# Attention core: the odd head's softmax rows normalised on GpSimd, the even head's on VectorE

## The chip, the cores and the metric

One NeuronCore of one Trainium2 chip runs the whole program. The metric is device time in microseconds (us) of one launch; the runs shown are compared by their median. The engines are TensorE (PE in the rows; PEld is its weight load), VectorE (DVE), ScalarE (ACT), GpSimd (POOL) and SyncE (SP), which here only issues transfers.

## What is computed

A two-layer encoder over 272 tokens (16 learned meta tokens and 256 others) of 1024 channels. Layer 0 holds grouped-query attention, layer 1 a recurrent block, and each is wrapped in two SwiGLU FFNs. The change lies in the attention of layer 0: 16 query heads of 64 channels, 4 key/value heads, full softmax over all 272 keys.

```
def attention_mixer(x, w_qkv, q_gain, k_gain, w_o, cos, sin):
    ...
    q = apply_rope(rms_norm(q, q_gain), cos, sin) * (HEAD_DIM ** -0.5)
    k = apply_rope(rms_norm(k, k_gain), cos, sin)
    def attend(qb):
        s = jnp.einsum('bqhgd,bkhd->bhgqk', qb, k).astype(jnp.float32)
        p = jax.nn.softmax(s, axis=-1).astype(v.dtype)
        return jnp.einsum('bhgqk,bkhd->bqhgd', p, v)
    ...
    return o @ w_o
```

## The kernel before

Every engine has its own written-out instruction stream, in order; semaphores tie them together. There is no scheduler: the order of the Python calls is the order on the engine.

The attention core is a loop of 18 steps (`STEPS`), nine for each pair of key/value heads. Step 0 and step 9 take the last 16 tokens of four head pairs at once and have one score tile of 128 rows by 272 keys; each of the other 16 steps takes 128 tokens of two heads, and so has two tiles, an even one and an odd one, which sit next to each other in `prow`, the SBUF buffer of the softmax rows. `prow` has four slots, two per step, used by turns. In all there are 34 tiles.

What one step s does, and where:

- TensorE `scores(s)` (L793): the scores into PSUM. From step 3 on it is issued two steps ahead, and waits until the exponents of step s-2 are out.
- VectorE `maximum(s)` (L1768) and `shifted(s)` (L1776): row maxima times the query's factor.
- ScalarE `exponents(s)` (L1292): one exponential per tile, from PSUM to `prow`, each with its row sum by an accumulator read.
- VectorE `inverse(s)` (L1781): the reciprocals `rinv` of the row sums of the step's tiles, one instruction; it raises the semaphore `p_inv`.
- VectorE `normalise(s)` (L1788): `prow` times `rinv`, one instruction per tile, each raising `p_norm`.
- TensorE `turn(s)` (L807): six small transposes per tile into PSUM. It waits on `p_norm` before each tile.
- ScalarE `place(s)` (L1314, L1308 for steps 0 and 9): copies the turned tiles to `pt`.
- TensorE `weigh(s)` (L819): the turned weights times the values. When the second half of a head pair is done, VectorE `out_split` (L1792, L1794) takes the result out of PSUM as a high part `xh` and a low part `xl`, and TensorE must wait for that (`o_ready`) before the next pair's first `weigh`.

The order on each engine: TensorE runs `scores(s+2)`, `turn(s)`, `weigh(s-1)`. ScalarE runs `exponents(s+1)`, `place(s)`. VectorE runs `normalise(s)`, then `out_split` in steps 4, 6, 8, 10, 13, 15 and 17, then `maximum(s+2)`, `inverse(s+1)`, `shifted(s+2)`. In steps 16 and 17 TensorE runs parts of the output projection (`begin_wo`) in place of scores. GpSimd does the rotary additions ahead of the core, and after it `restore(1)`, whose wait ends later; in the core it has no work.

Of the kernel before, what the change touches and what calls it, by code (L numbers as in the profile page):

```python
# [9 lines left out]
ALU = mybir.AluOpType  # L10
# [65 lines left out]
STEPS = NKV // 2 * STEPS_S  # L76
# [3 lines left out]
def first_tile(step):  # L80

    p, q = divmod(step, STEPS_S)
    return COLUMNS * p + max(0, 2 * q - 1)


def turning():
# [65 lines left out]
def build(nc, x, meta, gains, ffn_in, ffn_out, w_qkv, q_gain, k_gain, w_o, rec_in, conv_w, conv_b,  # L152
          gate_w, gate_b, lam, rec_out, consts, out):
    ctx = ExitStack()
    with ctx:  # L155
        def sb(name, shape, dt=F32):
            return ctx.enter_context(nc.sbuf_tensor(name, shape, dt))

        def sem(name):
            return ctx.enter_context(nc.semaphore(name))  # L160
# [40 lines left out]
        rinv = sb("rinv", [P, NKV // 2 * COLUMNS])  # L201
        prow = sb("prow", [P, 4, L])
# [47 lines left out]
        def row_parts(t):  # L250

            a = row_start(t)
            if t % 2:
                return (a, slice(0, 2 * P)), (a - META, slice(2 * P, L))
            return ((a, slice(0, L)),)
# [4 lines left out]


        gates_used = sem("gates_used")
        s_in, s_vec = sem("gains_landed"), sem("vectors_landed")
        table_loaded, warm_set = sem("table_loaded"), sem("warm_set")
        s_rope = sem("rotary_tables_landed")
# [16 lines left out]
        s_done, nmax_ready, p_exp, p_inv, p_norm, t_done, pt_ready, pv_done, oh_ready, o_ready = (sem(n) for n in (  # L282
            "s_done", "nmax_ready", "p_exp", "p_inv", "p_norm", "t_done", "pt_ready", "pv_done", "oh_ready", "o_ready"))
# [194 lines left out]
        def _(pe):  # L478
# [251 lines left out]
            def attention():  # L730
# [44 lines left out]
                def scores(s):  # L775

                    p, q = divmod(s, STEPS_S)
                    if s >= 2:
                        pe.wait_ge(p_exp, first_tile(s - 1))
                    dst = SCORE[s % 2]  # L780
                    if q == 0:
                        pe.wait_ge(q_roped, KT_N + 4 * p + 4)
                        for g in range(GROUP):
                            j, o = 2 * p + g // 2, HD * (g % 2)
                            last = pe.matmul(dst[32 * g:32 * g + 32, 0, 0:L], qt_row[o:o + HD, 2 * L * j + 2 * P:2 * L * j + 2 * P + 2 * META],
                                             kd[o:o + HD, j, :], start=True, stop=True)
                    else:
                        j, i, half = pair_of(s)
                        for keys in (slice(0, L // 2), slice(L // 2, L)):
                            for e in range(2):  # L790
                                o = HD * e
                                a = 2 * L * j + row_start(i) + P * half
                                last = pe.matmul(dst[:, e, keys], qt_row[o:o + HD, a:a + P],  # L793
                                                 kd[o:o + HD, j, keys], start=True, stop=True)
                    last.then_inc(s_done, 1)

                def turn(s):

                    banks, placed = TURN[s]
                    if placed:  # L800
                        pe.wait_ge(pt_ready, placed)
                    for e, tile in enumerate(range(first_tile(s), first_tile(s + 1))):
                        pe.wait_ge(p_norm, tile + 1)
                        for c, k0 in enumerate(KTOK):
                            for rows, b in zip((slice(0, HD), slice(HD, P)), banks):
                                o = HD * (3 * e + c)
                                last = pe.transpose(flipped[0:KT, b, o:o + HD], prow[rows, 2 * (s % 2) + e, k0:k0 + KT], ident[rows, rows])  # L807
                        last.then_inc(t_done, 1)
# [98 lines left out]
            def begin_wo(k0, k1):  # L907

                pe.wait_ge(w_ready, U_WO + 1)
                if k0 == 0:  # L910
                    pe.wait_ge(p_exp, first_tile(STEPS - 1))
                for k in range(k0, k1):
                    pe.wait_ge(o_ready, k + 1)
                    for m in range(2):
                        product(bank[PROJ_BANKS[1][0][m]][:, 0:L], U_WO, 2 * k + m, xh[:, k, :], xl[:, k, :], k == 0, False)
# [559 lines left out]
        def _(dve):  # L1475
# [214 lines left out]
            def attention():  # L1690
# [92 lines left out]
                def normalise(s):  # L1783
                    a, n = first_tile(s), first_tile(s + 1) - first_tile(s)
                    dve.wait_ge(p_inv, s + 1)
                    for e in range(n):
                        v = prow[:, 2 * (s % 2) + e, :]
                        dve.tensor_scalar(v, v, rinv[:, a + e:a + e + 1], None, ALU.mult).then_inc(p_norm, 1)  # L1788

                def out_split(pair):  # L1790
                    dve.wait_ge(pv_done, pair + 1)
# [215 lines left out]
        @block.gpsimd  # L2007
        def _(pool):
            def restore(n):

                t0 = PROJ_T0[n]
                pool.wait_ge(root_inverted, n)
                pool.wait_ge(x_ready, 8 * n + 8)
                pool.wait_ge(hsq_ready, 8 * n + 8)
                for c in range(KC):
                    pool.tensor_tensor(h[:, c, t0:L], h[:, c, t0:L], root[:, t0:L], ALU.mult).then_inc(h_restored, 1)  # L2016

            def rotary():
                def times_cos(t):
                    pool.wait_ge(q_gained, t + 1)  # L2020
                    if t >= 2:
                        pool.wait_ge(q_roped, t - 1)
                    pool.tensor_tensor(qc[:, t % 2, :], qp[:, t % 2, :], cos, ALU.mult).then_inc(q_cos, 1)

                def roped(t):
                    pool.wait_ge(q_sin, t + 1)
                    pool.wait_ge(q_cos, t + 1)
                    if t < KT_N:
                        last = pool.tensor_tensor(qn[:, t, :], qc[:, t % 2, :], pad[:, t % 2, 0:L], ALU.add)
                    for a, cols in row_parts(t) if t >= KT_N else ():  # L2030
                        a += 2 * L * ((t - KT_N) // 2)
                        n = cols.stop - cols.start
                        last = pool.tensor_tensor(qt_row[:, a:a + n], qc[:, t % 2, cols], pad[:, t % 2, cols], ALU.add)
                    last.then_inc(q_roped, 1)

                pool.wait_ge(s_rope, 16)
                pool.wait_ge(hacc_step, 8 * 1 + 8)
                for t in range(QKT):
                    times_cos(t)
                    if t == KT_N + 3:  # L2040
                        pool.wait_ge(q_final, KT_N)
                        pool.dma_start(kd[HD:P, 0:NKV:2, :], kd[0:HD, 0:NKV:2, :]).then_inc(k_dup, 16)
                        pool.dma_start(kd[0:HD, 1:NKV:2, :], kd[HD:P, 1:NKV:2, :]).then_inc(k_dup, 16)
                    roped(t)

            def recurrent():
                def gated_input(n):
                    for d in range(2):
                        pool.wait_ge(sig_done, 8 * n + 4 * d + 4)
                        v = gi[:, n % BLOCKS_HELD, d]  # L2050
                        pool.tensor_tensor(v, v, xc[:, n], ALU.mult).then_inc(ix_done, 1)

                def y_sum(n):
                    pool.wait_ge(scan_done, 4 * n + 4)
                    pool.tensor_tensor(ys[:, 2 * n:2 * n + 2, :], gw[:, n % BLOCKS_HELD, 0], gw[:, n % BLOCKS_HELD, 1], ALU.add).then_inc(ysum_done, 1)

                def y_gated(n):
                    pool.wait_ge(gelu_done, n + 1)
                    pool.wait_ge(ysum_done, n + 1)
                    s, t = slice(2 * n, 2 * n + 2), slice(PROJ_T0[4], L)  # L2060
                    pool.tensor_tensor(ys[:, s, t], ys[:, s, t], mg[:, s, t], ALU.mult).then_inc(y_full, 1)

                gated_input(0)
                gated_input(1)
                y_sum(0)
                gated_input(2)
                y_sum(1)
                y_gated(0)
                y_gated(1)
                gated_input(3)  # L2070
                y_sum(2)
                y_gated(2)

            rotary()
            restore(1)
            restore(2)
            restore(3)
            recurrent()
            restore(4)
# [26 lines left out]
```

## Time and profile before

| | us |
|---|---|
| median of 3 runs | 1049.96 (1049.76 to 1050.05) |
| the profiled execution, its own time | 1050.0 |
| its span | 1048.2 |
| PE busy (share of the span) | 1035.1 (99%) |
| DVE busy | 694.6 (66%) |
| ACT busy | 552.2 (53%) |
| POOL busy | 80.9 (8%) |

The granted TensorE clock was 0.999 of full speed. Busy time says how long an engine had an instruction in hand. In the timelines, a row begins with the start and the length; with "x2" the length is that of both together. Instructions of an engine are pipelined, so one may start a little before the row before it has ended. Brackets hold the idle time of the engine ahead of a row and who ended it. The attention core runs from about 268 to 300 us, and what is left of it overlaps the output projection up to 310 us.

### The profile page before, as it was taken

What the parts mean: (1) busy time and instruction counts of PE and PEld (TensorE: products, weight loads), DVE (VectorE), ACT (ScalarE), POOL (GpSimd) and SP (SyncE); (2) the same over time, 40 slices, a digit from 0 to 9 for tenths busy, and PEclk for the clock granted to TensorE, in tenths of its full rate; (3) what the DMA queues carried; (4) which work ended last, traced back from release to release, by engine and by line L of the source; (5) the groups of instructions that cost most, each with busy time, mean ns of one, the idle gap of its engine ahead of it and who ended that gap; (6) DMA issues with size and microseconds to landing.
All of it is one profiled execution on the core that took longest, in us unless ns stands there. A gap on an engine that the chain in (4) does not pass through costs nothing. (4 is left out here: it accounts for less than half of the span.)

```text
span 1048.2 us, 20625 instructions
## 1 busy us (share of the span) xinstructions
PE 1035.1 (99%) x8416; PEld 1010.2 (96%) x8416; DVE 694.6 (66%) x1008; ACT 552.2 (53%) x818; POOL 80.9 (8%) x76
## 2 busy tenths in 40 slices
PE   9999999999999999999999999999999999999997
PEld 8999999999789999999999999999999999999886
DVE  6766656478868866665487666554788687676652
ACT  6544454467875544444455444444568764544641
POOL 0000000008004000003000000030022320000000
PEclk9999999999999999999999999999999999999999
DMA  9654446635104365435746554466237426656531
GB/s 308 209 188 160 142 151 204 217 105 176 63 3 160 124 198 187 154 111 191 230 132 200 164 160 146 153 198 216 91 111 252 161 83 202 199 165 233 180 125 40
DMA packets 161200, 170.16 MB, mean 162 GB/s; under 512 B 3313, under 2 KB 154153, under 8 KB 161129
## 3 DMA queue, kind: packets, MB, share of 16 engines
q1 hardware_dynamic: 160744, 168.70, 49.5%
q8 instruction: 51, 0.84, 0.3%
q0 software_dynamic: 96, 0.28, 0.1%
q10 hardware_dynamic: 288, 0.18, 0.1%
q14 instruction: 21, 0.16, 0.0%
HBM read 167.82 MB, written 1.05 MB: 161 GB/s over the span
## 5 line engine op out<-in xcount | busy, mean ns | idle before, releaser
L1480 DVE TENSOR_TENSOR wl<-raw,wh 128x2048 fp32r<-128x2048 f32 (+2 forms) x164 | 342.4, 2108 | 147.1 <-ACT wh L1024 146.8
L483 PE MATMUL bank<-xh,wl 128*128 128x272 f32 (+1 forms) x1492 | 431.8, 289 | 0.1
L485 PE MATMUL bank<-xh,wh 128*128 128x272 f32 (+1 forms) x1492 | 428.6, 287 | 0.0
L484 PE MATMUL bank<-xl,wh 128*128 128x272 f32 (+1 forms) x1492 | 427.1, 286 | 0.0
L1024 ACT ACTIVATE wh<-raw 128x2048 fp32r<-128x2048 f32 (+3 forms) x163 | 280.4, 1744 | 107.7 <-PE bank L485 82.1
L483 PEld LDWEIGHTS bank<-xh,wl 128*128 128x128 f32 x1492 | 281.1, 188 | 1.9 <-issue 1.2
L485 PEld LDWEIGHTS bank<-xh,wh 128*128 128x128 f32 x1492 | 281.1, 188 | 0.0
L484 PEld LDWEIGHTS bank<-xl,wh 128*128 128x128 f32 x1492 | 281.1, 188 | 0.0
L484 PE MATMUL bank<-al,wh 128*128 128x272 f32 x528 | 152.2, 288 | 0.0
L483 PE MATMUL bank<-ah,wl 128*128 128x272 f32 x528 | 152.2, 288 | 0.0
L485 PE MATMUL bank<-ah,wh 128*128 128x272 f32 x528 | 151.4, 287 | 0.0
L1102 ACT ACTIVATE tmp<-tmp 128x272 f32<-128x272 f32 (+1 forms) x88 | 37.5, 427 | 207.3 <-DVE tmp L1575 207.1
L484 PEld LDWEIGHTS bank<-al,wh 128*128 128x128 f32 x528 | 99.3, 188 | 0.0
L485 PEld LDWEIGHTS bank<-ah,wh 128*128 128x128 f32 x528 | 99.2, 188 | 0.0
L483 PEld LDWEIGHTS bank<-ah,wl 128*128 128x128 f32 x528 | 99.2, 188 | 0.0
L1594 DVE TENSOR_TENSOR al<-tmp,ah 128x272 f32 (+3 forms) x88 | 38.2, 438 | 51.7 <-ACT ah L1107 51.1
L1575 DVE TENSOR_TENSOR tmp<-bank,r 128x272 f32<-128x272 f32 (+1 forms) x88 | 38.0, 432 | 45.3 <-PE bank L485 45.2
L2016 POOL TENSOR_TENSOR h<-h,root 128x272 f32<-128x272 f32 (+1 forms) x32 | 35.5, 1144 | 419.9 <-DVE root L1512 419.9
L1107 ACT ACTIVATE ah<-tmp 128x272 f32 (+3 forms) x88 | 37.4, 429 | 47.7 <-DVE tmp L1584 47.7
L1584 DVE TENSOR_TENSOR tmp<-tmp 128x272 f32<-128x272 f32 (+1 forms) x88 | 38.2, 437 | 13.9 <-ACT tmp L1102 11.5
L504 PE MATMUL bank<-xh,wl 128*128 128x272 f32 (+1 forms) x172 | 44.9, 289 | 1.2 <-ACT xh L1030 1.0
L505 PE MATMUL bank<-xh,wh 128*128 128x272 f32 (+1 forms) x172 | 44.5, 287 | 0.0
(206 smaller groups left out, 1146.4 us busy)
## 6 DMA issues: line engine op xcount, KB each, us to landing
raw<-in_ffn_w_in SPq DMA_DIRECT2D x87, 1024.0 KB, 5.3
raw<-in_ffn_w_out SPq DMA_DIRECT2D x24, 768.0 KB, 4.6
raw<-in_ffn_w_out SPq DMA_DIRECT2D x24, 640.0 KB, 3.9
raw<-in_ffn_w_out SPq DMA_DIRECT2D x10, 1024.0 KB, 5.2
raw<-in_rec_w_in SPq DMA_DIRECT2D x8, 1024.0 KB, 5.5
raw<-in_attn_w_qkv SPq DMA_DIRECT2D x6, 1024.0 KB, 5.0
raw<-in_attn_w_o SPq DMA_DIRECT2D x4, 1024.0 KB, 5.6
raw<-in_rec_gate_w SPq DMA_DIRECT2D x16, 256.0 KB, 5.1
```

Of the source, the lines that this page charges most:

```text
L483: pe.matmul(dst, b, mh, start=first, stop=False)
L484: pe.matmul(dst, a, ml, start=False, stop=False)
L485: return pe.matmul(dst, a, mh, start=False, stop=last)
L504: pe.matmul(dst, b, xh[:, k, t0:L], start=k == 0, stop=False)
L505: pe.matmul(dst, a, xh[:, k, t0:L], start=False, stop=False)
L1024: act.activation(wh[:, slot(u), 0:kn * 256], raw[:, slot(u), 0:kn * 256], ACT.Copy).then_inc(wh_ready, units)
L1102: act.activation(sl[:, b, t0:L], gp[:, b, t0:L], ACT.Silu).then_inc(silu_done, 1)
L1107: act.activation(ah[:, m, t0:L] if isinstance(it, int) else ah[:, bass.ds(4 * it + m, 1), t0:L].rearrange("p a l -> p (a l)"), aa[:, b, t0 ...
L1480: dve.tensor_tensor(wl[:, slot(u), 0:kn * 256], w, wh[:, slot(u), 0:kn * 256].bitcast(F32), ALU.subtract).then_inc(w_ready, units)
L1575: dve.tensor_tensor(gp[:, b, t0:L], bank[banks[0]][:, t0:L], r[:, t0:L], ALU.mult).then_inc(gate_scaled, 1)
L1584: dve.tensor_tensor(aa[:, b, t0:L], sl[:, b, t0:L], up[:, b, t0:L], ALU.mult).then_inc(a_full, 1)
L1594: dve.tensor_tensor(d, aa[:, b, t0:L], s, ALU.subtract).then_inc(a_ready, 1)
```

## The change

`normalise(s)` on VectorE now does only the even tile, and counts steps in `p_norm`. A new function on GpSimd, `normalise_odd(s)`, does the odd tile of the 16 steps that have one; it waits for the same `p_inv`, and raises a semaphore of its own, `p_norm_odd`. TensorE's `turn(s)` waits for `p_norm` before the even tile's six transposes and for `p_norm_odd` before the odd tile's six. The two buffers, the arithmetic and the order of everything else are as before. GpSimd runs all its 16 instructions between the rotary part and `restore(1)`.

```
+def odd_tiles(steps):
+    return first_tile(steps) - steps
...
                     for e, tile in enumerate(range(first_tile(s), first_tile(s + 1))):
-                        pe.wait_ge(p_norm, tile + 1)
+                        if e == 0:
+                            pe.wait_ge(p_norm, s + 1)
+                        else:
+                            pe.wait_ge(p_norm_odd, odd_tiles(s + 1))
...
                 def normalise(s):
                     a, n = first_tile(s), first_tile(s + 1) - first_tile(s)
                     dve.wait_ge(p_inv, s + 1)
-                    for e in range(n):
-                        v = prow[:, 2 * (s % 2) + e, :]
-                        dve.tensor_scalar(v, v, rinv[:, a + e:a + e + 1], None, ALU.mult).then_inc(p_norm, 1)
+                    v = prow[:, 2 * (s % 2), :]
+                    dve.tensor_scalar(v, v, rinv[:, a:a + 1], None, ALU.mult).then_inc(p_norm, 1)
...
+            def normalise_odd(s):
+                if first_tile(s + 1) - first_tile(s) == 2:
+                    pool.wait_ge(p_inv, s + 1)
+                    v = prow[:, 2 * (s % 2) + 1, :]
+                    t = first_tile(s) + 1
+                    pool.tensor_scalar(v, v, rinv[:, t:t + 1], None, ALU.mult).then_inc(p_norm_odd, 1)
+
             rotary()
+            for s in range(STEPS):
+                normalise_odd(s)
             restore(1)
```

VectorE before, from the normalisation of step 4 (with its `out_split`) to that of step 6:

```order
L1788 TENSOR_SCALAR prow<-prow,rinv 128x272 x2
L1792 CAST xh<-weighed 128x272
L1794 TENSOR_TENSOR xl<-weighed,xh 128x272
L1768 TENSOR_REDUCE nmax<-score_even 128x2
L1781 RECIPROCAL rinv<-rsum 128x2
L1776 TENSOR_TENSOR shift<-nmax,hq 128x2
L1788 TENSOR_SCALAR prow<-prow,rinv 128x272 x2
L1768 TENSOR_REDUCE nmax<-score_odd 128x2
```

VectorE after, the same stretch (all line numbers are 8 or 9 higher):

```order
L1796 TENSOR_SCALAR prow<-prow,rinv 128x272
L1800 CAST xh<-weighed 128x272
L1802 TENSOR_TENSOR xl<-weighed,xh 128x272
L1777 TENSOR_REDUCE nmax<-score_even 128x2
L1790 RECIPROCAL rinv<-rsum 128x2
L1785 TENSOR_TENSOR shift<-nmax,hq 128x2
L1796 TENSOR_SCALAR prow<-prow,rinv 128x272
L1777 TENSOR_REDUCE nmax<-score_odd 128x2
```

One of the two multiplications of each step has gone from VectorE; nothing else has moved there. GpSimd after, from the end of the rotary part to `restore(1)`:

```order
L2031 TENSOR_TENSOR tmp<-tmp,cst 128x272 [waits q_roped,q_gained]
L2041 TENSOR_TENSOR qt<-tmp,pad 128x256 [waits q_cos,q_sin]
L2041 TENSOR_TENSOR qt<-tmp,pad 128x16
L2087 TENSOR_SCALAR prow<-prow,rinv 128x272 [waits p_inv] x16
L2024 TENSOR_TENSOR h<-h,root 128x272 [waits hsq_ready,x_ready,root_inverted]
```

The row with x16 is new; before, the additions of `restore(1)` followed the rotary part directly.

## Rows read from the trace of the kernel before

**Rows 1.** The page's first part: busy time, share of span, instructions.

```profile
PE 1035.1 (99%) x8416; PEld 1010.2 (96%) x8416; DVE 694.6 (66%) x1008; ACT 552.2 (53%) x818; POOL 80.9 (8%) x76
```

**Rows 2.** Busy by stretch: PE, PEld, DVE, ACT, POOL; PEclk, DMA share, GB/s.

```profile
272.80:282.40 9.60, 8.69 (x152) 7.47 (x152) 8.65 (x30) 9.44 (x26) 0.00 (x0) 1.00 0.01 3
272.80:300.40 27.60, 25.12 (x422) 20.64 (x422) 24.61 (x82) 25.91 (x73) 0.00 (x0) 1.00 0.01 2
300.40:310.00 9.60, 9.60 (x105) 8.43 (x104) 2.18 (x8) 4.67 (x8) 0.00 (x0) 1.00 0.01 2
```

**Rows 3.** ScalarE's timeline around steps 4 to 6: start, length, instruction.

```profile
276.43 0.59 ACT L1292 ACTIVATE prow<-score_odd,shift,hq 128x272 f32<-128x272 f32 x1
...
277.53 0.82 ACT L1314 ACTIVATE pt<-flipped 96x768 f32<-96x768 f32 x1
278.41 0.58 ACT L1292 ACTIVATE prow<-score_even,shift,hq 128x272 f32<-128x272 f32 x1
```

**Rows 4.** VectorE's timeline from the normalisation of step 4 to step 6's.

```profile
276.09 0.63 DVE L1788 TENSOR_SCALAR prow<-prow,rinv 128x272 f32<-128x272 f32 x2
276.64 0.43 DVE L1792 CAST xh<-weighed 128x272 fp32r<-128x272 f32 x1
277.10 0.44 DVE L1794 TENSOR_TENSOR xl<-weighed,xh 128x272 fp32r<-128x272 f32 x1
...
278.09 0.15 DVE L1781 RECIPROCAL rinv<-rsum 128x2 f32<-128x2 f32 x1
278.21 0.16 DVE L1776 TENSOR_TENSOR shift<-nmax,hq 128x2 f32<-128x2 f32 x1
278.29 0.63 DVE L1788 TENSOR_SCALAR prow<-prow,rinv 128x272 f32<-128x272 f32 x2
279.28 0.72 DVE L1768 TENSOR_REDUCE nmax<-score_odd 128x2 f32<-128x544 f32 x1 [0.36 <-PE score_odd L793]
...
280.12 0.63 DVE L1788 TENSOR_SCALAR prow<-prow,rinv 128x272 f32<-128x272 f32 x2
280.66 0.43 DVE L1792 CAST xh<-weighed 128x272 fp32r<-128x272 f32 x1
```

**Rows 5.** TensorE's timeline in the same cycle, and the core's last wait.

```profile
277.69 0.88 PE L819 MATMUL weighed<-pt,vt 96*64 96x128 f32 x12 [0.40 <-DVE xl L1794]
278.50 0.73 PE L793 MATMUL score_odd<-kd,qt 64*128 64x136 f32 x8
279.06 0.50 PE L807 MATMUL flipped<-cst,prow 64*96 64x64 f32 x12
279.50 0.96 PE L819 MATMUL weighed<-pt,vt 96*64 96x144 f32 x12
...
299.60 0.88 PE L819 MATMUL weighed<-pt,vt 96*64 96x128 f32 x12 [0.26 <-DVE xl L1794]
```

**Rows 6.** Line L1788 alone: durations in ns, min/median/max, and its span.

```profile
L1788 DVE TENSOR_SCALAR prow<-prow,rinv x34: 353/356/363, 268.5 to 302.1; 128x272 f32<-128x272 f32 x34
```

**Rows 7.** VectorE's timeline where GpSimd works beside it.

```profile
242.99 0.43 DVE L1724 TENSOR_TENSOR pad<-bank,cst 128x272 f32<-128x272 f32 x1
...
245.30 0.78 DVE L1713 TENSOR_TENSOR hq<-hq,rc_q 128x4 f32<-128x4 f32 x1
246.00 2.28 DVE L1480 TENSOR_TENSOR wl<-raw,wh 128x2048 fp32r<-128x2048 f32 x1
...
779.20 1.68 DVE L1857 TENSOR_SCALAR xc<-pad,vec_b 128x272 f32<-128x272 f32 x2
```

**Rows 8.** GpSimd's timeline at the same places.

```profile
243.50 0.90 POOL L2033 TENSOR_TENSOR qt<-tmp,pad 128x256 f32<-128x256 f32 x2 [2.67 <-DVE pad L1724]
...
245.29 0.77 POOL L2033 TENSOR_TENSOR qt<-tmp,pad 128x272 f32<-128x272 f32 x1
246.01 2.90 POOL L2023 TENSOR_TENSOR tmp<-tmp,cst 128x272 f32<-128x272 f32 x1
...
779.05 1.34 POOL L2051 TENSOR_TENSOR gi<-gi,xc 128x544 f32<-128x544 f32 x1 [7.99 <-ACT gi L1339]
```

More of the change, by code:

```diff
@@ L262, in build @@
         gates_used = sem("gates_used")
+        p_norm_odd = sem("odd_tile_normalised")
         s_in, s_vec = sem("gains_landed"), sem("vectors_landed")
```

## Prediction

> **What bounds the kernel now.** I first read the page's busy shares: TensorE is busy for 99% of the span [rows 1]. So nothing that VectorE, ScalarE or GpSimd does in this kernel counts, unless it shortens or lengthens a wait of TensorE. The second view is the busy time by stretch. In one part of the attention core TensorE is busy for 8.69 us of 9.60, and ScalarE for 9.44; over the whole core from 272.8 to 300.4 TensorE is busy for 25.12 of 27.60; from 300.4 us on for 9.60 of 9.60 [rows 2]. The core is thus the place where TensorE waits, and whatever is won or lost there moves the start of the output projection at 300.4 us by as much, and with it the end of the kernel.
>
> Third, the timelines of one cycle, to see which wait ends last. ScalarE's part of a step is two exponentials and a copy: exponential at 276.43, copy at 277.53, which is 1.10 later, and from copy to the next exponential 0.70 where nothing holds it. That is a floor of 1.80 us for a step. The next exponential came at 278.41, so this step took 1.98 [rows 3]. It was held by the row maximum's product `shift`, which ended at 278.21 + 0.16 = 278.37 [rows 4].
>
> Why was `shift` late? Steps with an `out_split` form a loop that runs through two steps. In step 4: normalise 276.09, cast 276.64, `xl` 277.10 and its end at 277.54 [rows 4]; TensorE, idle for 0.40, starts `weigh` at 277.69 and the next scores at 278.50, ending at 279.23 [rows 5]; VectorE, idle for 0.36, takes the maximum at 279.28, then the reciprocal, and normalises step 6 at 280.12 [rows 4]. The period is 280.12 - 276.09 = 4.03 us for two steps, against ScalarE's floor of 3.60. The two multiplications of `normalise` are in this loop, ahead of the cast. The last such wait is the 0.26 us at 299.60 [rows 5], right ahead of the projection.
>
> **What goes from VectorE.** One tile takes 0.356 us, two tiles 0.63 [rows 4, 6], so 0.63 - 0.36 = 0.27 us go in each of 16 steps, 4.3 us of VectorE time in all. Only six of the seven steps with an `out_split` have it on TensorE's path (4, 6, 8, 10, 13, 15; that of step 17 comes when TensorE has the projection's products to do). In the others VectorE has idle time, or ScalarE's floor holds.
>
> **What is late next.** In step 6 the cast cannot start before `weigh(4)` has ended: 279.50 + 0.96 = 280.46, and it started at 280.66 [rows 4, 5]. With some 0.05 us for the hand-over it may come at 280.51, so 0.15 of the 0.27 can be taken there and no more. Written as a loop on TensorE, from scores(7) to scores(9): 278.50 to the end of `weigh(4)` 1.96, hand-over 0.05, cast 0.46, `xl` 0.44, hand-over 0.15, `weigh(5)` 0.81. Sum 3.87 against 4.03: 0.16 us per two steps is all that this loop gives.
>
> **What comes to GpSimd.** No row shows a multiplication by a column of scalars there. Nearest rows: an addition of two 128x272 tiles takes 0.77 us, one of 128x544 1.34 [rows 8]; the difference is 0.57 for 272 columns, so about 0.20 is fixed. An upper bound in kind is hard to give: a form with a scalar operand could be slower than the two-tensor form. From below, VectorE's own 0.356 for this very tile [rows 6] bounds it. I take 0.5 to 0.77, since only one tensor is read, and work the sum with 0.77 and with 0.5; for the range I also price 1.2.
>
> The Trainium skill (GPSIMD Engine Reference, Engine selection) says that operations with one input run on GpSimd at roughly line rate, which would be an estimate of some 0.4 us for this tile; no row here shows it. By it the sum would come out at the favourable end below.
>
> **The hand-overs and the port.** GpSimd starts about 0.08 us after VectorE's result: 242.99 + 0.43 = 243.42, start 243.50 [rows 7, 8]. VectorE itself goes on from its reciprocal sooner: 278.09 + 0.15 = 278.24, normalise at 278.29 [rows 4], which is 0.05. So the even multiplication starts some 0.03 us ahead of the odd one. They can't run side by side. At 245.30 a VectorE instruction on 4 columns took 0.78, because GpSimd had started at 245.29; at 246.00 VectorE started 0.01 ahead, and the GpSimd addition behind it took 2.90 in place of 0.77 [rows 7, 8]. That multiplications by a scalar column are hit too shows at 779.20: two took 1.68 while a GpSimd instruction begun at 779.05 ran for 1.34 [rows 7, 8]; the two heads' multiplication rows are of the same kind and size. So I let the odd tile start when the even one is done. In the pair at 246 us GpSimd ended at 248.91, 0.63 after VectorE's end at 248.28, which makes 0.14 of its 0.77 overlap. The odd tile is then ready at 0.36 + 0.63 + 0.06 (to TensorE) = 1.05 us after the even one's start if it costs 0.77, and at 0.78 if it costs 0.5. Before it was ready at 0.63.
>
> **What this does to the transposes.** In step 5 the odd tile was ready at 278.29 + 0.63 = 278.92, and its six transposes are the second half of those that start at 279.06, that is at about 279.30 [rows 4, 5]. With 1.05 it is ready at 279.34, which is late by 0.04; with 0.78 it is early. So the loop is 3.91 to 3.87 us long, and 0.12 to 0.16 shorter than before. In steps where the normalisation starts close to its scores the same 1.05 makes the odd transposes up to 0.3 us late (step 2, step 11: multiplication at about the time at which scores start). `place` is then just in time, but `weigh` and the scores behind it on TensorE start 0.3 later, and the first `out_split` of each half, in steps 4 and 13, loses nearly all its gain.
>
> **The sum.** With 0.77: steps 4 to 8 give about 0.07 us, steps 13 and 15 together about 0.17; in all -0.24. With 0.5: the first steps give 0.24 and the next 0.10 before TensorE's loop takes over, and some 0.04 of it is lost again in step 8, so -0.30; the second half gives 0.27 in step 13 and 0.16 in step 15, -0.43; in all -0.73. I take the middle on the cautious side, -0.4 us. Nothing after 300.4 us depends on the odd tiles of steps 16 and 17: their transposes stand behind products of the projection there, over 2 us long. `restore(1)` waits for other work until long after. The profiled execution took 1050.0 us, with a span of 1048.2, and the median is 1049.96, so both sums agree to 0.04. Forecast: 1049.96 - 0.4 = 1049.6 us.
>
> **Rivals.** First, GpSimd gets the port first. The margin is 0.03 us, and the multiplication must first read its scalar, so it may ask for the port later than its start says. Then the even tile waits for about 0.62 us of GpSimd's 0.77 (the 4-column instruction: 0.78 less its own 0.16), and is done 1.05 us after the reciprocal in place of 0.68 for both tiles before. That is about +0.4 in each two-step cycle, since the cast stands behind it: six cycles, +2.4 us, with little change in the steps at ScalarE's floor. Time 1052.3; with a GpSimd instruction of 0.5 us, +0.1 per cycle, no loss to be seen. This is the case on the other side, and its point of decision is which of the two starts first, with a GpSimd multiplication above 0.7 us. Against it stand the two pairs of rows above, in which the start order decided down to 0.01 us. The Trainium skill (SBUF — State Buffer, Who interferes with whom) has it as a rule: an instruction of VectorE in a two-port mode and one of GpSimd exclude each other, and whichever issues first keeps the shared ports for the whole instruction. By that rule, the trace agrees: 1.68 us for two multiplications.
>
> Second, the GpSimd multiplication is slow, 1.2 us. Then the loop above is 0.43 longer than 3.91, so +0.3 against before in each of four cycles; and the steps at ScalarE's floor are caught as well: exponentials to reciprocal to odd tile to transposes to copy to exponentials is about 3.6 us for two steps at 0.77 and 4.0 at 1.2, which costs 0.4 in each of three such pairs. Sum about +2.4, time 1052.4. From about 0.9 us on the change brings nothing.
>
> Third, nearly all of TensorE's idle time in the core goes. It is 27.60 - 25.12 = 2.48 us [rows 2], so a gain that can be seen, over 2.1 us, would have to take it nearly whole, the waits at ScalarE's floor with it. Time 1047.8; I give it little.
>
> **How the numbers follow.** A measurement of this kernel can tell about 0.2%, 2.1 us, from no change. My case, within 1 us of before, has 0.60. GpSimd first has 0.20, half of it beyond +2.1 us. The slow multiplication has 0.17, also half of it beyond. The whole gain has 0.03. That makes faster by over 0.2% 0.03, slower 0.19, and 0.78 within. The likeliest case alone spans 1049.1 to 1050.2. For 8 in 10 the range must reach into both slow cases, and leaves out their far ends: 1048.9 to 1052.3.
>
> **What would show it.** Right: L1796 at 18 instructions of 0.36 us; 16 GpSimd multiplications that start at VectorE's and last 0.9 at most, its wait included; the pair from normalise to the cast shrunk from 0.55 to 0.3; the period from step 4 to step 6 at 3.9; the projection's first product at 300.0 in place of 300.4. Wrong: even multiplications of 0.8 or more (GpSimd first), transposes that wait for GpSimd by more than 0.1 in most steps, or GpSimd rows above 1.2 us.

## The result

The changed kernel takes 1051.16 us (median of 20 runs, 1050.88 to 1053.59) against 1049.93 of the kernel before (20 runs, 1049.33 to 1050.44): ratio 1.0013, 95% interval 1.0007 to 1.0019. It is 1.2 us slower. The forecast was 0.4 us faster: the time lies in the stated range of 1048.9 to 1052.3, but the sign is the wrong one, and the likeliest case did not come.

The profiled execution took 1051.19 us with a span of 1049.4. The page's first part, to be read against [rows 1]:

```profile
PE 1036.2 (99%) x8416; PEld 1010.6 (96%) x8416; DVE 690.8 (66%) x992; ACT 552.8 (53%) x818; POOL 101.5 (10%) x92
```

VectorE lost 16 instructions, as worked out, and 3.8 us where 4.3 was worked out. GpSimd gained 16 instructions and 20.6 us; the 16 rows themselves make 17.9 of it, and the gate multiplications of layer 1, far behind the core, the other 2.7 (14.7 in place of 12.0). The two multiplication lines of the changed kernel (ns, min/median/max):

```profile
L1796 DVE TENSOR_SCALAR prow<-prow,rinv x18: 354/358/568, 268.4 to 303.0; 128x272 f32<-128x272 f32 x18
L2087 POOL TENSOR_SCALAR prow<-prow,rinv x16: 963/1131/1134, 269.5 to 303.0; 128x272 f32<-128x272 f32 x16
```

The second line is the answer in short. GpSimd needs 0.96 us for the odd tile where it starts first (step 4 alone), and 1.13 where it starts behind VectorE (the other 15). The median of VectorE's even multiplication stayed at 0.36, so GpSimd does not hold VectorE up in most steps. TensorE's timeline, at step 2 and from step 5 on, answers to [rows 5]:

```profile
272.90 0.38 PE L816 MATMUL flipped<-cst,prow 64*96 64x64 f32 x6 [0.46 <-ACT pt L1323]
273.64 0.37 PE L816 MATMUL flipped<-cst,prow 64*96 64x64 f32 x6 [0.36 <-POOL prow L2087]
273.94 0.88 PE L828 MATMUL weighed<-pt,vt 96*64 96x128 f32 x12
...
278.83 0.73 PE L799 MATMUL score_odd<-kd,qt 64*128 64x136 f32 x8
279.40 0.84 PE L816 MATMUL flipped<-cst,prow 64*96 64x64 f32 x12
280.17 0.96 PE L828 MATMUL weighed<-pt,vt 96*64 96x144 f32 x12
...
301.58 0.40 PE L489 MATMUL bank<-xh,wl 128*128 128x272 f32 x1
```

In step 2 the twelve transposes fall apart into six and six, with GpSimd named between them. In step 5 they take 0.84 in place of 0.50, and `weigh(4)` starts 1.34 us after the scores instead of 1.00. The projection's first product comes at 301.58; before it came at 300.41. Where the core begins on the time axis differs by up to 0.3 us between the traced executions, ahead of all that the change touches, so from here on I count from the core's first normalisation, that of step 0:

```profile
268.52 0.36 DVE L1788 TENSOR_SCALAR prow<-prow,rinv 128x272 f32<-128x272 f32 x1
300.41 0.39 PE L483 MATMUL bank<-xh,wl 128*128 128x272 f32 x1
```

before, and in the changed kernel

```profile
268.36 0.36 DVE L1796 TENSOR_SCALAR prow<-prow,rinv 128x272 f32<-128x272 f32 x1
```

From there to the projection it is 31.89 us before and 33.22 in the changed kernel: 1.33 us more, so the whole loss lies in the core. Counted in the same way, the normalisation comes 0.56 us later in step 4, 0.95 in step 9, 0.94 in step 10 and 1.30 in step 13. So about 0.9 of the 1.33 us arise at the start of the two halves (steps 2 to 4 and 11 to 13), and 0.4 in the cycles of the first half.

VectorE's timeline from step 4 to step 6, against [rows 4], and GpSimd's:

```profile
276.17 0.16 DVE L1790 RECIPROCAL rinv<-rsum 128x2 f32<-128x2 f32 x1
...
276.49 0.57 DVE L1796 TENSOR_SCALAR prow<-prow,rinv 128x272 f32<-128x272 f32 x1
276.98 0.43 DVE L1800 CAST xh<-weighed 128x272 fp32r<-128x272 f32 x1
...
278.43 0.15 DVE L1790 RECIPROCAL rinv<-rsum 128x2 f32<-128x2 f32 x1
278.55 0.16 DVE L1785 TENSOR_TENSOR shift<-nmax,hq 128x2 f32<-128x2 f32 x1
278.63 0.36 DVE L1796 TENSOR_SCALAR prow<-prow,rinv 128x272 f32<-128x272 f32 x1
...
280.45 0.36 DVE L1796 TENSOR_SCALAR prow<-prow,rinv 128x272 f32<-128x272 f32 x1
281.17 0.44 DVE L1800 CAST xh<-weighed 128x272 fp32r<-128x272 f32 x1 [0.36 <-PE weighed L828]
```

```profile
276.42 0.96 POOL L2087 TENSOR_SCALAR prow<-prow,rinv 128x272 f32<-128x272 f32 x1 [1.11 <-DVE rinv L1790]
278.68 1.13 POOL L2087 TENSOR_SCALAR prow<-prow,rinv 128x272 f32<-128x272 f32 x1 [1.30 <-DVE rinv L1790]
```

VectorE did get its time back, and now spends it waiting: before the cast at 281.17 it stands idle for 0.36 us, because `weigh(4)`, pushed back by the odd transposes, has not ended. From cast to cast the cycle lasts 281.17 - 276.98 = 4.19 us; before, 280.66 - 276.64 = 4.02 [rows 4]. Two waits, summed over the kernel (engine, what it waited for: us in total, times, longest), show the exchange. In the changed kernel:

```profile
PEld flipped L816 <- POOL prow L2087: 1.9, 6, 0.5
PE weighed L828 <- DVE xl L1802: 0.2, 1, 0.2
```

and before:

```profile
PE weighed L819 <- DVE xl L1794: 1.4, 4, 0.5
```

The wait for `xl` fell from 1.4 us to 0.2. In its place the transposes' weight loads wait 1.9 us for GpSimd. (Not all of either is lost time: what counts is the 1.33 us by which the core is longer.)

### The profile page after: what moved, and what is told of

The parts are those of the page before. It is cut to its first block and busy times, and to the rows that moved or that the text cites. A ratio compares the mean times of both kernels' runs of the same rounds, so it can differ in the third digit from the quotient of the medians.

```text
span 1049.4 us, 20625 instructions
## 1 busy us (share of the span) xinstructions
PE 1036.2 (99%) x8416; PEld 1010.6 (96%) x8416; DVE 690.8 (66%) x992; ACT 552.8 (53%) x818; POOL 101.5 (10%) x92
## 3 DMA queue, kind: packets, MB, share of 16 engines
HBM read 167.82 MB, written 1.05 MB: 161 GB/s over the span
```

## The experiments

Three theories were to be told apart. *Late tile*: GpSimd delivers the odd tile too late. *Port*: VectorE and GpSimd hold each other up. *Hand-over*: the second semaphore and the split wait themselves cost something. The comparison in each case is with the kernel before, run on the same chip in the same job (1049.89, 1049.84 and 1049.81 us in the three jobs). The intervals of most of these single comparisons are some 0.9 us to either side, so for differences below 1 us I also take from the trace the stretch from the core's first normalisation to the projection's first product (31.89 us before). It rests on one execution of each kernel. All diffs are against the changed kernel.

**Semaphores alone.**

```
                     dve.tensor_scalar(v, v, rinv[:, a:a + 1], None, ALU.mult).then_inc(p_norm, 1)
+                    if n == 2:
+                        v = prow[:, 2 * (s % 2) + 1, :]
+                        dve.tensor_scalar(v, v, rinv[:, a + 1:a + 2], None, ALU.mult).then_inc(p_norm_odd, 1)
...
-            for s in range(STEPS):
-                normalise_odd(s)
```

> VectorE does both tiles again, one instruction each, but the odd one raises its own semaphore and TensorE waits on two semaphores in turn; GpSimd does nothing in the core. Late tile (the loss comes from when GpSimd delivers the odd tile): as before, 1049.9, within 0.2 us. Port (VectorE and GpSimd block each other): also as before. Hand-over (the second semaphore and the split wait cost something themselves): about 1051, as the change.

Measured: 1050.06 us, ratio 1.0001 (0.9992 to 1.0010), and the stretch is 31.91 us against 31.89. The hand-over costs nothing that can be seen.

**The odd tile left out.**

```
-                        else:
-                            pe.wait_ge(p_norm_odd, odd_tiles(s + 1))
...
-            for s in range(STEPS):
-                normalise_odd(s)
```

> The odd tile is not normalised at all, so that half of the weights keep their row sums; VectorE does the even tile alone and TensorE waits for nothing else. This is the change with a multiplication on GpSimd that costs nothing. Late tile: the gain of the shorter VectorE chain stands alone, between 0.4 and 0.9 us faster than before, about 1049.2. If the shorter chain is worth nothing, 1049.9. Hand-over and port say nothing here.

Measured: 1049.32 us, ratio 0.9995 (0.9986 to 1.0004). The time alone does not prove a gain; the trace has a stretch of 31.34 us (268.44 to 299.78), 0.55 shorter than before, which agrees with the medians (0.57):

```profile
299.78 0.40 PE L489 MATMUL bank<-xh,wl 128*128 128x272 f32 x1
```

So the shorter VectorE chain is worth about 0.6 us when no odd tile is late. One part of the gain is missing even here: in step 4 the even multiplication starts 0.32 us after its reciprocal has ended, in place of 0.04 before, and the cast comes no sooner than before. In this kernel GpSimd has no work, so it is not GpSimd's doing:

```profile
275.81 0.17 DVE L1788 RECIPROCAL rinv<-rsum 128x2 f32<-128x2 f32 x1
...
276.30 0.36 DVE L1794 TENSOR_SCALAR prow<-prow,rinv 128x272 f32<-128x272 f32 x1 [0.24 <-issue]
```

**The odd tile left out, GpSimd busy beside.**

```
+        idle = sb("idle", [P, L])
...
-                        else:
-                            pe.wait_ge(p_norm_odd, odd_tiles(s + 1))
...
+                    pool.wait_ge(idle_step, odd_tiles(s) + 1)
-                    pool.tensor_scalar(v, v, rinv[:, t:t + 1], None, ALU.mult).then_inc(p_norm_odd, 1)
+                    pool.tensor_scalar(idle[:, :], idle[:, :], rinv[:, t:t + 1], None, ALU.mult).then_inc(idle_step, 1)
```

> As the run without the odd tile (which stays unnormalised), but GpSimd multiplies a tile of the same size that nobody reads, at the same moments and with the same scalar column. Late tile: within 0.3 us of the run without the odd tile, since nobody waits for GpSimd. Port: as slow as the change, about 1051, since VectorE's instructions are held up in the same way.

Measured: 1049.60 us, ratio 0.9998 (0.9989 to 1.0007). Its two lines show the same load on GpSimd as in the change, and VectorE hardly touched:

```profile
L1796 DVE TENSOR_SCALAR prow<-prow,rinv x18: 354/358/416, 268.4 to 301.2; 128x272 f32<-128x272 f32 x18
L2087 POOL TENSOR_SCALAR idle<-idle,rinv x16: 962/1132/1135, 269.6 to 301.3; 128x272 f32<-128x272 f32 x16
```

The stretch is 31.39 us, 0.05 more than without GpSimd. So what GpSimd does to VectorE in this form costs between 0.05 (trace) and 0.3 us (medians), and what is left, from 1049.60 to the change's 1051.16, is TensorE's wait for the tile. That does not clear the port: of the 1.13 us after which the tile is ready, 0.17 are what GpSimd loses behind VectorE, and the next runs show what 0.17 us are worth there.

**Less and more of the tile.** Half of the columns:

```
-                    v = prow[:, 2 * (s % 2) + 1, :]
+                    v = prow[:, 2 * (s % 2) + 1, 0:L // 2]
```

> GpSimd multiplies only the left 136 of the odd tile's 272 columns; the right half stays unnormalised. Its instruction should take about 0.6 us in place of 0.96. Late tile: the odd tile is ready 0.4 us sooner, the transposes wait in hardly any step, and the time falls to 1049.3 to 1049.7. Port: VectorE is held up only where GpSimd starts first, and the time falls by less than 0.3 us from 1051.2.

204 columns, the same edit with `0:204`:

> GpSimd multiplies the left 204 of the odd tile's 272 columns; the rest stays unnormalised. By the two sizes measured the instruction takes 0.82 us alone and 0.99 behind VectorE's, which is what the prediction had put in for the whole tile. Late tile, with the prediction's sum: 1049.6 to 1049.8. If the loss grows from the first tenth of lateness on, halfway between the half tile and the change, about 1050.3.

Half a tile more:

```
+                    pool.tensor_scalar(v[:, 0:L // 2], v[:, 0:L // 2], rinv[:, t:t + 1], None, ALU.mult).then_inc(idle_step, 1)
+                    pool.wait_ge(idle_step, odd_tiles(s) + 1)
                     pool.tensor_scalar(v, v, rinv[:, t:t + 1], None, ALU.mult).then_inc(p_norm_odd, 1)
```

> As the change, but ahead of each odd tile GpSimd also multiplies the left half of that tile by itself (that half is then normalised twice), so that the tile is ready about 0.65 us later. Late tile: each of the 14 steps in the loop is held by TensorE's wait for GpSimd; the two-step period grows by about 0.65, in all 4 to 7 us more than the change, 1055 to 1058. Port: VectorE's own instructions are held a little more, under 1 us more.

Measured, with the time from GpSimd's start to the tile's end behind a VectorE that started first (for the last row 271.56 - 269.71, two instructions), and with the stretch of the trace:

| odd tile on GpSimd | ready after (us) | time (us) | against before | stretch against 31.89 |
|---|---|---|---|---|
| none | - | 1049.32 | -0.57 | -0.55 |
| 136 columns | 0.79 | 1049.47 | -0.42 | -0.39 |
| 204 columns | 0.96 | 1050.11 | +0.30 | +0.43 |
| 272 columns (the change) | 1.13 | 1051.16 | +1.23 | +1.33 |
| 136 and 272 | 1.85 | 1055.35 | +5.51 | +5.37 |

The ratios of the three new kernels are 0.9996 (0.9987 to 1.0005), 1.0003 (0.9994 to 1.0012) and 1.0055 (1.0042 to 1.0069): of these times only the last is clear of before by itself; the other two rest on the trace beside them.

```profile
L2087 POOL TENSOR_SCALAR prow<-prow,rinv x16: 677/792/795, 269.5 to 301.3; 128x136 f32<-128x136 f32 x16
```

```profile
L2087 POOL TENSOR_SCALAR prow<-prow,rinv x16: 792/960/963, 269.7 to 302.2; 128x204 f32<-128x204 f32 x16
```

Up to 0.79 us nearly all of the gain is kept. From 0.96 on each 0.1 us of lateness costs some 0.6 us: (1055.35 - 1051.16) / (1.85 - 1.13) = 5.8, about one lateness per two-step cycle. This fits the loop in which the odd transposes stand once. The run with 204 columns also prices the port: it delivers after 0.96 us, when the whole tile would be ready if VectorE did not stand in its way, and is 1.05 us faster than the change. By this estimate most of the change's 1.23 us hang on the last 0.17. Late tile and port are thus one chain: VectorE delays GpSimd, and GpSimd's tile delays TensorE. In the slowest of these kernels the wait for GpSimd is the long one:

```profile
PEld flipped L817 <- POOL prow L2090: 6.7, 11, 1.2
```

**Another form on GpSimd.**

```
-                    pool.tensor_scalar(v, v, rinv[:, t:t + 1], None, ALU.mult).then_inc(p_norm_odd, 1)
+                    pool.tensor_tensor(v, v, rinv[:, t:t + 1].broadcast_to([P, L]), ALU.mult).then_inc(p_norm_odd, 1)
```

> As the change, but GpSimd multiplies the odd tile by a two-tensor multiplication whose second operand is the scalar column broadcast along the row. If that form takes the 0.77 us of the additions, the odd tile comes 0.2 us sooner than in the change. Late tile: the time falls to about 1049.7 to 1050.3. Port: a form that reads two tensors from SBUF blocks VectorE no less; no change from 1051.2, or slower.

Measured: 1051.51 us, ratio 1.0015 (1.0006 to 1.0024). The expectation by the late tile failed, though its premise was more than met: the instruction takes 0.64 us. What it does to VectorE is in the other line, and in the two rows of step 5:

```profile
L2087 POOL TENSOR_TENSOR prow<-prow,rinv x16: 638/640/641, 269.4 to 303.2; 128x272 f32<-128x272 f32 x16
L1796 DVE TENSOR_SCALAR prow<-prow,rinv x18: 355/835/842, 268.2 to 303.2; 128x272 f32<-128x272 f32 x18
```

```profile
278.52 0.83 DVE L1796 TENSOR_SCALAR prow<-prow,rinv 128x272 f32<-128x272 f32 x1
```

```profile
278.56 0.64 POOL L2087 TENSOR_TENSOR prow<-prow,rinv 128x272 f32<-128x272 f32 x1 [1.76 <-DVE rinv L1790]
```

GpSimd is recorded 0.04 us after VectorE, takes its full speed, and VectorE is held for 0.48. So it goes in 15 of the 16 steps; in step 4 GpSimd starts 0.08 ahead and VectorE takes 0.71. To see whether this hold is the whole loss, the same form multiplied a tile that nobody reads, with the odd tile left out (the third experiment with the two-tensor form in it):

> The odd tile stays unnormalised and nobody waits for GpSimd, which beside it multiplies a tile of the same size in the two-tensor form. Port: the form holds VectorE's even multiplication for 0.84 us in place of 0.36 in nearly every step, as it did where it made the odd tile, and the time is about 1051.0 to 1051.5, nearly all of that run's loss. Late tile: VectorE's delay is hidden, and the time is below 1050.

Measured: 1051.61 us, ratio 1.0020 (1.0011 to 1.0029), VectorE's median again 835 ns, and the core is as long as in the run before it (33.64 against 33.62 us). With this form the port is the whole loss, and nobody needs to wait for GpSimd to have it.

**GpSimd only where VectorE has an `out_split` next.**

```
+def by_pool(step):
+    return step < STEPS - 1 and step >= 2 and (step - 2) % STEPS_S and pair_of(step - 2)[2] and first_tile(step + 1) - first_tile(step) == 2
...
+                            if by_pool(s):
+                                pe.wait_ge(p_norm_pool, len([i for i in range(s + 1) if by_pool(i)]))
+                            else:
+                                pe.wait_ge(p_norm_odd, odd_tiles(s + 1) - len([i for i in range(s) if by_pool(i)]))
...
+                    if n == 2 and not by_pool(s):
+                        v = prow[:, 2 * (s % 2) + 1, :]
+                        dve.tensor_scalar(v, v, rinv[:, a + 1:a + 2], None, ALU.mult).then_inc(p_norm_odd, 1)
...
-                if first_tile(s + 1) - first_tile(s) == 2:
+                if by_pool(s):
```

> GpSimd takes the odd tile only in the six steps whose normalisation stands ahead of an out_split on VectorE (4, 6, 8, 10, 13, 15); in the ten others VectorE does both tiles, as before. Late tile: in those six steps TensorE waits for xl anyway, so the late tile is hidden, and in the steps where it was exposed (2, 3, 5, 7, 11, 12, 14) it is back to 0.63; time 1049.2 to 1049.7, 0.3 to 0.7 faster than before. Port: half of the change's loss stays, about 1050.5.

Measured: 1049.66 us, ratio 0.9997 (0.9988 to 1.0007): the change's loss is gone, a gain is not shown. In the trace the stretch is 31.70 us, 0.19 shorter than before. Step 4 shows why it is no more:

```profile
276.73 0.33 PE L824 MATMUL flipped<-cst,prow 64*96 64x64 f32 x6
277.27 0.37 PE L824 MATMUL flipped<-cst,prow 64*96 64x64 f32 x6 [0.21 <-POOL prow L2098]
277.58 0.88 PE L836 MATMUL weighed<-pt,vt 96*64 96x128 f32 x12
```

Counted from the core's start (268.43 here), `xl` is ready 0.24 sooner, but the odd tile keeps TensorE, and `weigh` starts at 9.15 us where it started at 9.17 before [rows 5]. With the two-tensor form in the same six steps:

> As the run before it, with the two-tensor form on GpSimd. Late tile: as that run or 0.1 to 0.2 faster, if the form is the quicker one.

Measured: 1050.88 us, ratio 1.0010 (1.0001 to 1.0019), the stretch 32.78: slower, against the expectation. VectorE's even multiplication takes 0.84 in just those six steps, and the cast stands behind it.

## Why the prediction was wrong

The step that failed first is the term for GpSimd's multiplication: 0.5 to 0.77 us in the sum, 0.96 measured. With it failed the price of a late tile: the sum had nothing for the stop of the transposes, and let the first `out_split` of each half come out even.

- **What bounds the kernel, and what VectorE gives up**: right. The core is longer by 1.33 us, the kernel by 1.23. One tile went from each of 16 steps, and the shorter chain is worth about 0.6 us where the odd tile costs nothing; the prediction had 0.73 for its best case. What is missing from the 0.73 is about the late start in step 4, where the prediction had a gain and the run without the odd tile has none. That `weigh(4)` would be the next thing in the way of the cast was right too: it is the idle time at 281.17.
- **The duration on GpSimd** is the term that failed first. I took 0.5 to 0.77 us, "since only one tensor is read". It is 0.96, and 1.13 behind VectorE. The three sizes alone, 0.68, 0.79 and 0.96 us for 136, 204 and 272 columns, give 2.1 ns a column, as the two-tensor rows had in [rows 8] (0.57 us for 272); what differs is the fixed part, 0.39 us in place of 0.20. Reading one tensor less saved nothing in this form; what the extra 0.19 is spent on, no run tells. The row I chose by kind was a lower bound, not an upper one. (Of those rows the 128x544 one and the one of 2.90 us are multiplications of two tiles, L2051 and L2023, which the prediction calls additions; its numbers stand.)
- **The port term** was right in size. The sum let GpSimd end 0.14 us sooner than one whole instruction after the other; by that, 0.96 gives 0.36 + 0.96 - 0.14 = 1.18 us from VectorE's start, and 0.05 + 1.13 = 1.18 was measured. So all of the excess in this term is the 0.19 by which 0.96 is more than 0.77. The prediction's loop of 3.91 us becomes 4.10 with it, already longer than the 4.03 of before. From cast to cast 4.19 was measured.
- **The sum itself** failed too. With 204 columns GpSimd delivers 0.05 + 0.96 = 1.01 us after VectorE's start, which is what the sum had for its cautious end (0.36 + 0.63 = 0.99), and yet the trace has the core 0.43 us longer where the sum had a gain of 0.24. Two things were missing. First, the stop costs more than the lateness: six transposes that had to wait take 0.30 us until `weigh` starts (273.64 to 273.94), against about 0.20 in a row of twelve. In that kernel the odd tile of step 5 was late by some 0.05 us (279.55 and 0.06 to TensorE, against half of the transposes at about 279.56), and `weigh(4)` came 0.15 later than in flow. The same 0.1 is what lacks between the 4.10 and the 4.19 above:

```profile
278.59 0.96 POOL L2087 TENSOR_SCALAR prow<-prow,rinv 128x204 f32<-128x204 f32 x1 [1.41 <-DVE rinv L1790]
```

```profile
279.32 0.67 PE L816 MATMUL flipped<-cst,prow 64*96 64x64 f32 x12
279.91 0.96 PE L828 MATMUL weighed<-pt,vt 96*64 96x144 f32 x12
```

  Second, the first `out_split` of a half. I had let the 0.27 us saved in step 4 pay for 0.3 us of lateness handed on from step 2, so that nothing would be lost there. Counted from the core's start (268.49 in this kernel), step 4's maximum comes 0.41 us late, since it waits for the scores, and its cast 0.28. The terms of the 0.28: the reciprocal 0.29 late, the late start of the multiplication 0.11, 0.16 because GpSimd had started ahead and held it (0.52 in place of 0.36), less the 0.27 saved; they add up to 0.29. The saving did pay; the late start and GpSimd's hold were not in the sum. Before:

```profile
275.12 0.72 DVE L1768 TENSOR_REDUCE nmax<-score_odd 128x2 f32<-128x544 f32 x1 [0.22 <-PE score_odd L793]
275.88 0.17 DVE L1781 RECIPROCAL rinv<-rsum 128x2 f32<-128x2 f32 x1
```

and with 204 columns:

```profile
275.50 0.72 DVE L1777 TENSOR_REDUCE nmax<-score_odd 128x2 f32<-128x544 f32 x1 [0.88 <-PE score_odd L799]
276.14 0.16 DVE L1790 RECIPROCAL rinv<-rsum 128x2 f32<-128x2 f32 x1
...
276.46 0.52 DVE L1796 TENSOR_SCALAR prow<-prow,rinv 128x272 f32<-128x272 f32 x1
276.89 0.43 DVE L1800 CAST xh<-weighed 128x272 fp32r<-128x272 f32 x1
```

- **The second rival, a slow multiplication**, is what happened, though milder: it put +2.4 us at 1.2 us and nothing at 0.9. At 0.96 the kernel lost 1.2, so its point of decision lay too high, for the same two reasons. The chances gave this rival 0.17 and my case 0.60. The range held the time because it reached up for the two rivals, not because my case was near.
- **The first rival, the port**, came true in one step only of the change: in step 4 GpSimd started 0.07 ahead and VectorE took 0.57. With the two-tensor form it came true in full. By the rival's own way of counting, that form should cost six times the 0.21 us by which its even tile (done 0.05 + 0.84 = 0.89 after the reciprocal) comes later than 0.68, that is +1.3 us; +1.7 to +1.8 was measured.
- **The rule on the order of starts** did not hold as I used it. The prediction said that the start order decides down to 0.01 us. With the two-tensor form GpSimd started some 0.04 later in 15 of 16 steps and got the port each time. The Trainium skill (SBUF — State Buffer, Who interferes with whom) puts it down to which issues first; the recorded starts of these rows do not tell that order. The exclusion itself agrees with this form: 0.48 us of hold on VectorE beside a GpSimd instruction of 0.64. With the scalar-column form it is not seen for the whole instruction: in step 4 of the change VectorE ended at 277.06, 0.32 us before the end of the GpSimd multiplication that had started ahead of it.
- **The Trainium skill's rule** (GPSIMD Engine Reference, Engine selection) that one-input operations run on GpSimd at roughly line rate is not borne out here: by the clock that page gives, 1.2 GHz, and one column per cycle, 272 columns would be an estimated 0.23 us, and 0.57 is measured from the slope.

What remains open: why in step 4 the even multiplication starts 0.16 us after its reciprocal has ended in place of 0.04, which lets GpSimd in. It is late, by 0.16 to 0.32 us, in all eight traced kernels in which VectorE does only one tile in steps 1 to 3, among them the one in which GpSimd has no work; it is on time, at 0.03 to 0.04, in the four in which it does two there. No run looked for the cause.

## What to carry to other kernels

Work taken from the busy engine is worth only what the next wait in the loop leaves (here 0.6 us of 4.3), while the helper's result must be on time in every step. So compare the moment at which the helper delivers, hand-over and port wait included, with the moment at which its reader wants it, before counting what the busy engine saves. A slower helper does no harm where the reader is held by something else anyway, as in the six steps with an `out_split` (0.19 us shorter in the trace, a gain in time not shown), and even there only if it does not hold the busy engine's own instruction. And where two engines get in each other's way, count what the helper loses as well: 0.17 us on GpSimd cost about 1 us here.

## What the runs showed of the hardware

- A multiplication by a scalar column on GpSimd, f32, 128 partitions: 0.68, 0.79 and 0.96 us for 136, 204 and 272 columns; with the column broadcast as the second tensor of a two-tensor form, 0.64 us for 272. A multiplication of two full tiles there takes 0.76 (the rotary part of the kernel before):

```profile
240.07 0.76 POOL L2023 TENSOR_TENSOR tmp<-tmp,cst 128x272 f32<-128x272 f32 x1
```

- The quicker form was the worse neighbour. Started 0.04 us behind VectorE's multiplication it held that for 0.48 us; the slower form, started 0.05 behind, held it for nothing and lost 0.17 itself. That the slower form asks for the port only after its longer fixed part would explain both, but not step 4 of the change, where it started only 0.07 ahead, lost nothing and held VectorE for 0.21; this was not tried apart.
- Six transposes that follow a wait delay what comes behind them by about 0.1 us more than the wait itself (0.30 in place of 0.20 from their start to `weigh`).
